# First gate behind the attention as seven block products, with its branch's product ahead of it

## The reference

```python
o_a = multiscale_pool_mixer(u_pool, w_pool, pool_scale)
o_b = sliding_window_gqa_sinks(q, k, v, attn_sinks)
o_c = short_gated_conv(xc, gate_b, gate_c, conv_w)
gates = jax.nn.sigmoid(gate_logits).reshape(B, S, N_BRANCHES, D_MODEL)
merged = (gates[:, :, 0] * jnp.einsum('bsc,cd->bsd', o_a, w_branch_a)
          + gates[:, :, 1] * jnp.einsum('bsc,cd->bsd', o_b, w_branch_b)
          + gates[:, :, 2] * jnp.einsum('bsc,cd->bsd', o_c, w_branch_c))
mix = jnp.einsum('bsd,de->bse', merged, w_o)
x = layer_norm(ALPHA * x + mix, ln1_g, ln1_b)
```

## Time and profile before

| | us |
|---|---|
| median of 3 runs | 2817.7 |
| lowest, highest | 2817.55, 2818.31 |
| the profiled execution | 2818.4 |
| its span | 2816.6 |
| TensorE busy in it | 2796.8 |
| VectorE, ScalarE busy | 1689.3, 1760.8 |

### The profile page before, as it was taken

One profiled execution on the slowest core, in us unless ns is written; L12 is line 12 of the kernel. 1 busy time (PEld: TensorE's weight loads), 2 busy tenths in 40 slices (PEclk: granted clock), 3 DMA queues, 4 the chain that ended last, 5 costly groups with the idle time before them and its releaser, 6 DMA issues.

```text
span 2816.6 us, 42829 instructions
## 1 busy us (share of the span) xinstructions
PE 2796.8 (99%) x15818; PEld 2442.9 (87%) x15818; DVE 1689.3 (60%) x2977; ACT 1760.8 (63%) x2565; POOL 408.2 (14%) x472
## 2 busy tenths in 40 slices
PE   9999999999999999999999999999999999999999
PEld 7989899889998688899988898799987889789997
DVE  6654637254553773644446675678748766657865
ACT  7666767565655774666656755666656765666664
POOL 1111111111111001111111111111111011111110
PEclk9999999999999999999999999999999999999999
DMA  9776767688888327888885688888887578798884
GB/s 249 163 151 143 170 130 176 144 194 189 191 185 197 78 59 178 188 195 188 190 196 131 142 191 191 178 178 192 197 194 166 114 170 187 172 201 181 192 196 112
DMA packets 137038, 481.72 MB, mean 171 GB/s; under 512 B 15344, under 2 KB 15600, under 8 KB 136720
## 3 DMA queue, kind: packets, MB, share of 16 engines
q0 software_dynamic: 67296, 227.77, 45.8%
q1 hardware_dynamic: 68688, 249.59, 30.0%
q10 hardware_dynamic: 864, 1.78, 0.2%
HBM read 476.99 MB, written 2.10 MB: 170 GB/s over the span
## 4 chain that ended last, share of the span: by engine, by line
PE 97%; DVE 1%; ACT 1%; issue 0%; DVEq 0%; ACTq 0%
PE ps L1500 48%; PE ps L1676 24%; PE ps L1519 5%; PE ps L1952 3%; PE ps L2022 3%; PE ps L2091 2%; PE ps L1619 1%; PE ps L2116 1%; PE ps L1889 1%; PE ps L2138 1%; PE ps L1474 1%; PE ps L1796 1%; PE ps L1580 1%; PE ps L1602 0%; PE ps L1878 0%; PE ps L1577 0%
## 5 line engine op out<-in xcount | busy, mean ns | idle before, releaser
L563 ACT ACTIVATE wh<-raw 128x1024 fp32r<-128x1024 f32 (+2 forms) x461 | 455.4, 988 | 566.6 <-PE ps L1500 427.5
L546 POOL DMA_DIRECT2D wl<-weights x465 | 406.4, 874 | 2373.0 <-ACT wl L568 2313.0
L568 ACT ACTIVATE wl<-raw 128x1024 fp32r<-128x1024 f32 (+2 forms) x461 | 450.7, 978 | 0.0
L1500 PE MATMUL ps<-HH,wh 128*128 128x512 f32 x1088 | 427.3, 393 | 0.7 <-issue 0.5
L1500 PE MATMUL ps<-HH,wl 128*128 128x512 f32 x1088 | 423.8, 390 | 0.0
L1500 PE MATMUL ps<-HL,wh 128*128 128x512 f32 x1088 | 423.6, 389 | 0.0
L1500 PE MATMUL ps<-MH,wh 128*128 128x512 f32 x928 | 362.3, 390 | 0.7 <-DVE ML L2800 0.7
L1500 PE MATMUL ps<-MH,wl 128*128 128x512 f32 x928 | 361.3, 389 | 0.0
L1500 PE MATMUL ps<-ML,wh 128*128 128x512 f32 x928 | 361.1, 389 | 0.0
L1500 PEld LDWEIGHTS ps<-HH,wh 128*128 128x128 f32 x1088 | 204.3, 188 | 45.1 <-issue 3.4
L1500 PEld LDWEIGHTS ps<-HH,wl 128*128 128x128 f32 x1088 | 204.2, 188 | 43.0
(11 more groups left out here) (448 smaller groups left out, 5682.7 us busy)
## 6 DMA issues: line engine op xcount, KB each, us to landing
raw<-weights SPq DMA_DIRECT2D x468, 512.0 KB, 5.0
wl<-weights POOLq DMA_DIRECT2D x329, 512.0 KB, 7.8
wl<-weights POOLq DMA_DIRECT2D x136, 384.0 KB, 6.6
XT<-x SPq DMA_DIRECT2D x4, 512.0 KB, 8.4
out<-XT SPq DMA_DIRECT2D x3, 512.0 KB, 2.6
arena<-tables POOLq DMA_DIRECT2D x1, 1024.0 KB, 11.0
arena<-table_h ACTq DMA_DIRECT2D x1, 640.0 KB, 5.8
arena<-swaps_a POOLq DMA_DIRECT2D x1, 576.0 KB, 8.4
```

The lines of the kernel that those rows point to most:

```text
L546: pool.dma_start(wl[:, n, first:], weights[slab][:, first:], accum_op=ALU.add).then_inc(w_lo[n], 16)
L563: act_f(wh[:, n, at:w], raw[:, n, at:w], ACT.Copy)
L568: act_f(wl[:, n, at:w], raw[:, n, at:w], ACT.Identity, scale=-1.0).then_inc(w_hi, 1)
L1500: op = mm(bank(g, t), w[:, slot, at:at + P], x[:, first + kt, :], start=(kt == 0 and w is wh and x is xh), stop=(kt == n_k - 1 and w is wl ...
```

## The change

In both hybrid layers, gate (0,1) becomes a seven-product gate too. Branch b's product goes ahead of it: TensorE makes branch a's product, branch b's, then the two sets of the gate (0,1), then those of (0,2). The slabs are laid out in that order in memory, and the semaphore counts and unit numbers move with it.

On ScalarE, the product of branch b is copied from PSUM to `sg`. The gate's sigmoids are written in place into `gate_out`. On VectorE, `weighed(0)` and `weighed(1)` multiply the halves of `sg` by them, each ahead of the next `twist_sums`, and one addition of 2048 columns a partition adds `sg` to `mg` (`weighed_added`), behind the low parts of gate (0,2)'s units and ahead of its first sums. The high and low parts of the four input sums are made in the order 2, 0, 1, 3, all before the gate. In the attention's last three steps with `exp_heads` (13 to 15), and behind them, `high(i-3)` stands behind `exp_heads(i)` instead of ahead of it.

```diff
--- before.py
+++ after.py
@@ -94,10 +94,11 @@
 H_STEPS = 16
+GX_ORDER = (2, 0, 1, 3)
 HALVES = (slice(0, 256), slice(256, 512))
...
 H_SUMS = sum(H_TWIST.values())
-H_GATES = ((0, 2), (1, 0), (1, 1), (1, 2))
+H_GATES = ((0, 1), (0, 2), (1, 0), (1, 1), (1, 2))
 H_LAYER = dict(slab=120, group=32 + 2 * len(H_PARTS) + H_SUMS + len(H_GATES) + 1, split=4 + 8 + 8 + 2 * UP_SETS + 8, att=16, hl=1, sq=16, ln=2, ts=2,
...
@@ -1154,7 +1156,7 @@
-def gate_twisted(k, before):
+def gate_twisted(k, free, kept=None):
...
@@ -1168,9 +1170,9 @@
 if i == 0:
-    wait_taken(act, before)
+    free()
 act.wait_ge(gt_sum, k + i + 1)
-act_f(sg[:, 2 * i:2 * i + 2, :], gate_out, ACT.Sigmoid).then_inc(gt_gate, 1)
+act_f(kept if kept is not None else sg[:, 2 * i:2 * i + 2, :], gate_out, ACT.Sigmoid).then_inc(gt_gate, 1)
...
@@ -1359,10 +1361,13 @@
     turned(i - 2)
-if i >= 3:
+late = i >= H_STEPS - 3
+if i >= 3 and not late:
     high(i - 3)
...
     exp_heads(i, a + i)
+if late:
+    high(i - 3)
 if i == H_STEPS + 1:
@@ -1387,24 +1392,27 @@
 for b, k in enumerate((1, 2, 1)):
-    if half or b:
-        before = c.at["group"] + (-1)
-        if (half, b) in H_GATES:
-            gate_twisted(10 * layer + 2 + 2 * H_GATES.index((half, b)), before)
-        else:
-            for m in range(1, 4):
-                gate_sum_high(layer, m)
-            g, last = set_of(4)
-            wait_used(act, last)
-            gate_sum_high(layer, 0)
-            wait_taken(act, before)
-            for t in range(4):
-                act_f(sg[:, t, :], bank(g, t), ACT.Sigmoid).then_inc(acc_free[g.mod(2)], 1)
-            for n in range(k):
-                gate_high(u0 + (4 + n))
-                set_slab()
-            c.take("group")
-            continue
+    before = c.at["group"] + (-1)
+    k0 = 12 * layer + 2
+    if (half, b) == (0, 1):
+        for m in GX_ORDER:
+            gate_sum_high(layer, m)
+        g, s = c.take("group"), c.take("slab", 2)
+        high_parts(s + 4, 1)
+        act.wait_ge(gx_done, 4 * layer + 1)
+        gate_high(2 * k0)
+        gate_high(2 * k0 + 1)
+        high_parts(s + 5, 1)
+        wait_used(act, s + 1)
+        wait_taken(act, before)
+        for t in range(4):
+            act_f(sg[:, t, :], bank(g, t), ACT.Copy).then_inc(acc_free[g.mod(2)], 1)
+        gate_twisted(k0, lambda: None, gate_out)
+        continue
+    if (half, b) == (0, 2):
+        gate_twisted(k0 + 2, lambda: act.wait_ge(gt_mixed, layer + 1))
+    elif half:
+        gate_twisted(k0 + 2 * H_GATES.index((half, b)), lambda: wait_taken(act, before))
     if half == 1 and b == 2:
...
@@ -2157,15 +2165,16 @@
     for b, (k, at, ready) in enumerate(branches):
-        if (half, b) in H_GATES:
-            first = 10 * layer + 2 + 2 * H_GATES.index((half, b))
-            if first == 10 * layer + 2:
-                pe.wait_ge(gx_done, 4 * layer + 4)
+        first = 12 * layer + 2 + 2 * H_GATES.index((half, b)) if half or b else None
+        if (half, b) == (0, 1):
+            pe.wait_ge(low_done, hl.times(H_STEPS).value(H_STEPS))
+            features(k, MH, ML, ready, first=at)
+            pe.wait_ge(gx_done, 4 * layer + 4)
+        if half or b:
             for i in range(2):
                 twist_set(first + i, gate_sums, True)
-        elif half or b:
-            features(4, HH, HL, nothing)
-        features(k, MH, ML, ready, first=at, each_bank=not half and not b)
+        if (half, b) != (0, 1):
+            features(k, MH, ML, ready, first=at, each_bank=not half and not b)
 s = c.take("split", KT)
...
@@ -2488,7 +2497,7 @@
-def gate_twisted(k):
+def gate_twisted(k, kept):
...
@@ -2509,6 +2518,9 @@
     dve.wait_ge(gt_gate, gates_made(k + i))
+if kept[i] is not None:
+    kept[i]()
+    dve.drain()
 twist_sums(k + i, tw_gate, gt_copied, gt_sum)
@@ -3226,26 +3238,37 @@
 for b, k in enumerate((1, 2, 1)):
-    twisted_gate = (half, b) in H_GATES
-    if twisted_gate:
-        at = 10 * layer + 2 + 2 * H_GATES.index((half, b))
-        gate_twisted(at)
-    elif half or b:
-        gg, _ = skip_set(4)
-        for m in range(1, 4):
-            gate_sum_low(4 * layer + m, m)
-        gate_raw(u0, hl_slab + 25)
-        gate_sum_low(4 * layer + 4, 0)
-        gate_raw(u0 + 1, hl_slab + 26)
-        for n in range(2):
-            gate_low(u0 + n)
-            gate_raw(u0 + n + 2, hl_slab + (27 + n))
+    at = 12 * layer + 2 + 2 * H_GATES.index((half, b)) if half or b else None
+    if (half, b) == (0, 1):
+        gg, _ = skip_set(k)
+        for n, m in enumerate(GX_ORDER):
+            gate_sum_low(4 * layer + n + 1, m)
+        dve.drain()
+        gate_low(u0)
+        gate_raw(u0 + 1, hl_slab + 22)
+        gate_low(u0 + 1)
+        gate_raw(u0 + 2, hl_slab + 23)
+        gate_raw(u0 + 3, hl_slab + 24)
+        wait_taken(dve, gg)
+        def weighed(i):
+            two = sg[:, 2 * i:2 * i + 2, :]
+            v.tensor_tensor(two, two, gate_out, ALU.mult)
+        def weighed_added():
+            weighed(1)
+            dve.drain()
+            v.tensor_tensor(mg[:, 0:4, :], mg[:, 0:4, :], sg, ALU.add).then_inc(gt_mixed, 1)
+        gate_twisted(at, (None, lambda: weighed(0)))
+        continue
+    if half or b:
+        gate_twisted(at, (weighed_added if (half, b) == (0, 2) else None, None))
     g, last = skip_set(k)
-    if twisted_gate:
+    if half or b:
         dve.wait_ge(gt_gate, gates_made(at + 2))
-    elif half or b:
-        wait_taken(dve, gg)
     else:
+        gate_raw(u0, hl_slab + 21)
         dve.wait_ge(gate_ready, hl.times(4).value(4))
@@ -3287,8 +3310,8 @@
 UP_TWISTED = [at + 6 * first + j for at in H_AT for first, sets in H_TWIST.items() for j in range(4 * sets)]
-GATE_UNITS = [at - 54 + first + j for at in H_AT for first in (10, 25, 30, 35, 41) for j in range(4)]
-UNITS = 20
+GATE_UNITS = [at - 54 + first + j for at in H_AT for first in (10, 21, 25, 30, 35, 41) for j in range(4)]
+UNITS = 24
@@ -3359,8 +3382,9 @@
     for b in range(3):
-        out.append((twisted_slabs if (half, b) in H_GATES else lambda w: slabs(w, 512))(gates[:, b, at]))
-        out.append(slabs(branches[b][:, at], 512))
+        pair = ((twisted_slabs if (half, b) in H_GATES else lambda w: slabs(w, 512))(gates[:, b, at]),
+                slabs(branches[b][:, at], 512))
+        out.extend(pair[::-1] if (half, b) == (0, 1) else pair)
 out.append(slabs(a["w_o_2"][layer], 512))
```

More of the change, by code:

```diff
@@ L382, in block_program @@
         gt_hi, gt_low, gt_first, gt_copied = sem("gt_hi"), sem("gt_low"), sem("gt_first"), sem("gt_copied")
+        gt_mixed = sem("gt_mixed")
         gt_sum, gt_gate = sem("gt_sum"), sem("gt_gate")
@@ L469, in gates_made @@
         def gates_made(k):
-            return 8 * (k // 10) + k % 10 - 2
+            return 10 * (k // 12) + k % 12 - 2
         def raw_read(slab):
@@ L1300, in _ @@
                     high_parts(s + (4 + 2 * i), 1)
-                    act.wait_ge(gt_first, 10 * layer + i + 1)
+                    act.wait_ge(gt_first, 12 * layer + i + 1)
                     act_f(tw_conv[i][:, 5], tw_bank(g + i, 0)[:, 0], ACT.Copy).then_inc(gt_copied, 1)
@@ L2078, in _ @@
                 pe.wait_ge(gy_done, 4 * layer + 4)
-                twist_set(10 * layer, conv_sums, True, rotate_queries)
-                twist_set(10 * layer + 1, conv_sums, True)
+                twist_set(12 * layer, conv_sums, True, rotate_queries)
+                twist_set(12 * layer + 1, conv_sums, True)
                 gate, s = c.take("group"), c.take("slab", 4)
@@ L3126, in _ @@
                 rope(3)
-                twist_sums(10 * layer, tw_conv[0], gt_copied, gt_sum)
+                twist_sums(12 * layer, tw_conv[0], gt_copied, gt_sum)
                 gate_low(u0 + 3)
-                twist_sums(10 * layer + 1, tw_conv[1], gt_copied, gt_sum)
+                twist_sums(12 * layer + 1, tw_conv[1], gt_copied, gt_sum)
                 gate, _ = skip_set(4)
```

## The result

The changed kernel takes 2824.99 us (median of 13 runs, 2822.53 to 2828.63), the kernel before 2818.48 on the same chip (13 runs, 2816.73 to 2822.27). The ratio is 1.0022 with a 95% interval of 1.0015 to 1.0029: 6.2 us slower, 4.2 to 8.2. The forecast, 2.5 us slower with an upper end of 2823.0, had the sign right and was too small by more than half. The two profiled executions differ by 5.1 us: spans of 2816.6 and 2821.7.

What follows compares the result with a forecast made beforehand. VectorE was taken to bound X already, by a hair. X later by 0.9 and 0.7 us plus 0.9 for stray gaps made +2.5 us on the median of 2817.7: 2820.2 us, range 2817.4 to 2823.0.

Steps and rivals of the forecast that it cites:

- What bounds the kernel: TensorE is busy 99% of the span, but X is already bound by VectorE's last sums of gate (0,2), by a hair.
- X: First product of gate (1,0), waiting for VectorE's last sums of gate (0,2); forecast 0.9 us later in second layer, 0.7 in first.
- TensorE's part: Gate (0,1) with seven products takes 19.74 us instead of 21.75: 2.01 us less per layer if nothing else ends last.
- The tail: Attention's end, where TensorE waited 0.75 us for VectorE: 0.4 us gained per layer, bounds 0.7 and -0.2.
- The new waits: TensorE ahead of gate (0,1): `low_done` costs nothing, low parts come 0 to 0.5 us late, absorbed if X waits.
- The list: VectorE's and ScalarE's steps from the last low part, 2258.8, to the fourth sums' end, 2321.4, second layer.
- stray gaps: VectorE pauses of 0.44 and 0.45 us ahead of X; one per layer counted, 0.88 us in all, bounds none and three.
- Behind X nothing differs: After the first product of gate (1,0), VectorE stands as before with the sums just done; no further cost counted.
- A: Rival: ScalarE and VectorE turns overlap 3.3 us more per layer, X ready with TensorE; 4.8 us gained, 2812.9; chance 0.08.
- B: Rival: raw slab 26 lands late for ScalarE, delaying list and X; at 10 us landing 2823.4; chance 0.11 with its like.
- C: Rival: the Trainium skill's matmul spacing holds, TensorE reaches X 7.2 us later than by the rows; 2828.0; chance 0.01.
- D: Rival: X doesn't move, the list being 0.9 us shorter; 2817.7; chance 0.80 together with the forecast.

Runs made afterwards that it cites:

- e6: Changed kernel with one low part of 1024 columns ahead of the fourth sums made twice on VectorE: 2827.41 us, ratio 1.0034.
- e5: Changed kernel without the long addition (one column instead of 2048, so the first half's output lacks branch b): 2817.56 us, ratio 0.9995.
- e4: Changed kernel with `high(i - 3)` ahead of the exponentials again in the attention's last steps: 2825.03 us, ratio 1.0022.
- e7: Kernel before with only the new order of exponentials and high parts at the attention's tail: 2817.76 us, ratio 0.9998.
- e1: The changed kernel run again, unedited, beside the kernel before: 2824.19 us, ratio 1.0025.
- e8: Changed kernel with only the second half of the long addition put behind the fourth sums: 2821.61 us, ratio 1.001.
- e2: Changed kernel with 12 idle TensorE products ahead of branch c's product in each hybrid layer, filling the wait: 2821.57 us, ratio 1.0011.
- e10: Changed kernel with the long addition on GpSimd and the low part of X's second unit behind the fourth sums: 2819.88 us, ratio 1.0002.
- e3: Changed kernel with the low part of X's second unit and half the long addition put behind the fourth sums: 2818.94 us, ratio 1.0005.
- e9: Changed kernel with the long addition of 2048 columns made by GpSimd instead of VectorE: 2824.43 us, ratio 1.0019.

## Why the prediction was wrong, point by point

**What bounds the kernel: right.** X was bound by VectorE's list, one to one (e6: 1.24 us in, 1.24 us out; e5: some 2.25 taken, 2.14 gained).

**TensorE's part: right in size.** 19.75 us for the gate, 2.00 saved for each layer, all of it absorbed by the wait at X. The estimate from the Trainium skill's spacing (17.8 us) stays refuted.

**The tail: right.** 0.3 us for each layer (e4, e7), taken as 0.4. TensorE's wait of 0.75 us became one of 0.24 for a copy.

**The new waits: right.** `low_done`, `gx_done` and `gt_low` show none in the view of waits between 2260 and 2324 us.

**The list: right to 0.3 us.** VectorE in the second layer, for the earlier trace rows:

```profile
2260.54 0.29 DVE L3218 TENSOR_TENSOR ML<-arena,MH 128x128 fp32r<-128x128 f32 x1 [2.37 <-ACT MH L1355]
...
2279.01 1.23 DVE L2480 TENSOR_TENSOR arena_r<-arena,arena_r 128x1024 fp32r<-128x1024 f32 x1 [1.13 <-ACT arena_r L1150]
...
2309.15 2.29 DVE L3261 TENSOR_TENSOR arena<-arena 128x2048 f32<-128x2048 f32 x1
...
2322.73 0.69 DVE L2541 TENSOR_TENSOR arena<-arena,ps 128x512 f32<-128x512 f32 x1
```

From the last low part to the end of the fourth sums it is 2323.42 - 2260.54 = 62.9 us; the list said 2321.4 - 2258.8 = 62.6. The long addition took 2.29 us, as taken. X comes 1.22 us later than before in the second layer, for 0.9, and the list's 0.3 us more make the difference; in the first layer 1.02, for 0.7 and a gap. Of the two stray gaps taken, one is there (0.42 us of "issue" at 1615.70, first layer); the second layer has none over 0.2. So X's two terms and the gaps, 2.5 together, measured 1.22 + 1.02 = 2.24: the near agreement is partly luck, a gap too many against a list too short. The wait at X, 3.25 us for 3.3, is luck in part too: counted from the joint, X and TensorE's readiness both came 0.4 us later than forecast (2321.85 for 2321.5, 2318.6 for 2318.2 on the clock of before).

**The step that failed: "Behind X nothing differs".** It looked at VectorE only. TensorE itself runs at the lower clock level behind a wait of 3.25 us, which cost 1.6 and 1.3 us in the profiled execution, and 2.8 in e1's first layer, where the level stayed down longer. That term stood at zero and measured 2.9 us for both layers. With X's 2.24 it makes the 5.17 of the two layers (2.57 + 2.60), and the forecast's own 2.5 with it would have been 5.4, inside the measured 4.2 to 8.2. The prediction had used the clock one sentence too early: a pause of 0.75 us at the tail "has not lowered it", and it then created one of over four times that length without asking again. The profile of before had a warning: near 953 us the clock is at its lower level, 2 to 6 us behind waits of 1.62 (946.40) and 0.46 us (950.49), with small products between; an earlier one of 0.70 us ends at 934.38. What of this lowered it is not shown. Stretch 950.50 to 955.00 of before, then of after, where the same waits stand ahead of it:

```profile
950.50:955.00 4.50, 4.50 (x22) 3.17 (x23) 1.43 (x3) 1.86 (x6) 0.23 (x1) 0.73 0.99 210
```

```profile
950.50:955.00 4.50, 4.50 (x32) 3.89 (x33) 2.30 (x7) 2.44 (x7) 0.22 (x1) 1.00 0.92 198
```

**The rivals.** A (the list not dense) fell: VectorE is busy for 56.14 of the 62.88 us, and of the rest 1.9 us are waits for ScalarE's high parts, as the list had them; the remainder is drains and short gaps. B (raw slab 26) fell: no wait of ScalarE for a load. C fell. D (X not moved) fell by 1.2 us. None of them had the clock, so the range, made of them, ended at 2823.0. What is left open: by medians after and before differ by 6.5 us, 1.3 more than the 5.2 that the traces show between the joints, which is inside the interval; and why of two equal waits (e8) one is followed by the lower level.

## What to carry to other kernels

Where TensorE gets its work done sooner and another engine then ends last, the saving turns into one wait, and a wait of some us has a second price: the matmuls behind it start at half the clock, under a profile that shows TensorE as busy. Here that was so behind one of two waits of 2.2 us and behind all of 2.8 us and more, at 1.3 to 2.8 us each; price it beside the wait itself, and look at the granted clock of a short stretch right behind it. A few idle products that run while TensorE would wait buy that back (e2), but they don't make the late engine any sooner. Work taken off that engine altogether kept its full worth here (e5); work put behind the sums that TensorE waited for kept it as long as it was one step of 1.2 us (e8, e10), and came back in part as new waits when it was two (e3).

## What the hardware showed that was not expected

The lower clock level doesn't lessen TensorE's busy time and is hidden in the page's tenths: the mean clock of a run, by its median, moves only from 0.999 (before, e2, e3, e5, e7, e10) to 0.998 (after, e1, e4, e8, e9) and 0.997 (e6). The same waits give the lower level in one execution and not in another (near 953 us, and in e8 one layer and not the other), which can be part of why runs of one kernel differ: e1's lie within 5.4 us of each other, e2's within 3.1, and of the 21 runs of before beside e9 the three over 2822 us have a mean clock of 0.998, the other 18 one of 0.999 or 1.000. And GpSimd, idle for 86% of the span, is no free adder beside a busy VectorE: 4.82 us for an addition that takes 2.29, and 1.6 us of VectorE's time lost to it.
